# Linear attention of the third layer: a tile's head products moved into the next tile's two passes

## What is computed

```python
def gla_scan(q, k, v, loga, s0):
    ...
        b = jnp.cumsum(ac, axis=2)
        diff = b[:, :, :, None, :] - b[:, :, None, :, :]
        decay = jnp.exp(jnp.where(mask, diff, -jnp.inf))
        attn = jnp.einsum('bhid,bhjd,bhijd->bhij', qc, kc, decay)
        o = attn @ vc + jnp.einsum('bhid,bhde->bhie', qc * jnp.exp(b), S)
    ...
    o = o_f + flip(o_b)
    o = o * lax.rsqrt(jnp.mean(o * o, axis=-1, keepdims=True) + EPS)
    o = o.transpose(0, 2, 1, 3).reshape(B_, L, GLA_VAL_WIDTH) * g_gla.astype(jnp.float32)
    o = (o * jax.nn.silu(r.astype(jnp.float32))).astype(h.dtype)
```

## Time and profile before

| | us |
|---|---|
| median of 3 runs (4013.52 to 4015.33) | 4013.7 |
| the profiled execution | 4014.44 |
| its span | 4012.6 |
| PE busy in it | 3857.4 |
| DVE busy in it | 2246.1 |
| ACT busy in it | 828.2 |
| POOL busy in it | 602.2 |

### The profile page before, as it was taken

How to read it: one execution, slowest core, us unless ns; L and a number is a source line. 1 busy time by engine, 2 the same in 40 slices (tenths; PEclk the granted TensorE clock), 3 DMA queues, 4 the chain that set the end, 5 groups by cost and what they waited for, 6 DMA issues and landing times.

```text
span 4012.6 us, 45750 instructions
## 1 busy us (share of the span) xinstructions
PE 3857.4 (96%) x17426; PEld 2301.8 (57%) x17426; DVE 2246.1 (56%) x3730; ACT 828.2 (21%) x1615; POOL 602.2 (15%) x944
## 2 busy tenths in 40 slices
PE   8999999999999999999999998899999999999998
PEld 5676455544455555458744645645555444758863
DVE  0375533466566655544556016737687765438876
ACT  1265211100122222112101014521100012531000
POOL 1000000133231441400132002200000430000023
PEclk9999999999999999999999998999999999999999
DMA  5354121354412222312344112411112552002234
GB/s 190 114 203 168 32 63 53 127 178 168 141 64 74 95 69 68 126 54 94 126 168 152 58 42 93 167 38 53 63 53 75 177 179 70 9 23 84 95 126 162
DMA packets 209782, 410.57 MB, mean 102 GB/s; under 512 B 5938, under 2 KB 92296, under 8 KB 209440
## 3 DMA queue, kind: packets, MB, share of 16 engines
q1 hardware_dynamic: 203712, 386.94, 28.1%
q0 software_dynamic: 5856, 20.73, 1.7%
HBM read 405.49 MB, written 2.16 MB: 102 GB/s over the span
## 4 chain that ended last, share of the span: by engine, by line
PE 88%; DVE 6%; ACT 3%; DMA 1%; issue 1%; POOL 0%; DVEq 0%; ACTq 0%; SPq 0%; POOLq 0%
PE PS L1206 28%; PE PS L1301 19%; PE PS L1166 5%; PE PS L1139 3%; PE PS L1768 3%; PE PS L1117 3%; PE PS L1782 3%; PE PS L909 2%; PE PS L1769 1%; PE PS L1929 1%; PE PS L1939 1%; PE PS L1407 1%; PE PS L1119 1%; PE PS L1616 1%; PE PS L1418 1%
## 5 line engine op out<-in xcount | busy, mean ns | idle before, releaser
L1206 PE MATMUL PS<-UT,RING 128*128 128x384 f32 (+1 forms) x2432 | 693.8, 433 | 10.7 <-ACT BIG L2998 9.6
L1206 PEld LDWEIGHTS PS<-UT,RING 128*128 128x128 f32 x2432 | 460.9, 190 | 205.5 <-issue 15.5
L1206 PE MATMUL PS<-BIG,RING 128*128 128x384 f32 (+1 forms) x1824 | 528.5, 433 | 0.8 <-DVE BIG L2833 0.5
L1206 PEld LDWEIGHTS PS<-BIG,RING 128*128 128x128 f32 x1824 | 346.0, 190 | 147.2 <-DVEq L2004 1.1
L1301 PE MATMUL PS<-RING,BIG 128*128 128x512 f32 x810 | 377.3, 593 | 3.8 <-POOL RES_TMP L3598 1.4
L3593 POOL TENSOR_TENSOR RES_TMP<-BIG 128x128 f32<-128x128 f32 x68 | 35.7, 525 | 1668.5 <-DVE BIG L2839 581.3
L2682 DVE TENSOR_TENSOR RING<-RING 128x512 f32<-128x512 f32 x135 | 104.7, 776 | 276.5 <-DMA RING<-ff_w_dram 173.3
L1301 PEld LDWEIGHTS PS<-RING,BIG 128*128 128x128 f32 x810 | 151.2, 190 | 184.3 <-issue 177.1
L1301 PE MATMUL PS<-RING,GATE 128*128 128x512 f32 x536 | 243.9, 596 | 5.9 <-DVE RING L2685 5.9
L1301 PE MATMUL PS<-RING,RES_TMP 128*128 128x512 f32 x544 | 245.3, 593 | 1.4 <-DVE UT L2714 0.8
L1301 PEld LDWEIGHTS PS<-RING,GATE 128*128 128x128 f32 x536 | 102.0, 191 | 136.5 <-issue 125.4
(11 more groups left out here) (466 smaller groups left out, 5837.7 us busy)
## 6 DMA issues: line engine op xcount, KB each, us to landing
RING<-ff_w_dram SPq DMA_DIRECT2D x112, 1024.0 KB, 4.9
RING<-w_mod_dram SPq DMA_DIRECT2D x48, 2048.0 KB, 8.1
RING<-w_ffn_down_dram SPq DMA_DIRECT2D x55, 1024.0 KB, 5.0
RING<-w_ffn_up_dram SPq DMA_DIRECT2D x44, 1024.0 KB, 5.1
RING<-ssm_w_in_dram SPq DMA_DIRECT2D x8, 2048.0 KB, 7.8
RING<-ssm_w_out_dram SPq DMA_DIRECT2D x4, 2048.0 KB, 7.7
RING<-w_even_in_dram SPq DMA_DIRECT2D x4, 2048.0 KB, 8.6
GATE<-gates_dram POOLq DMA_DIRECT2D x12, 512.0 KB, 9.6
```

The costliest lines, as they stand in the source:

```text
L1206: m = mm(bank(bank_, n), a[:, k, :], b[:, k, :], start=k == 0, stop=k == 3)
```

## The change

`C_AT` becomes two buffers, used by even and odd tiles in turn: the old one, and `GATE[:, 1, 0, :]`. The heads of tile t are no longer one block after its second pass. They are four calls `head(t, h)` in the passes of tile t+1: after v2 and v4 of the first pass, and after v7 and v0 of the second; for tile 4 all four in the first pass of tile 5 (after v2, v3, v4, v5); for tile 5 they stay at the end. What depends on them moves later: `heads_scaled` and `heads_gated` of tile t-2 into the first pass of tile t, after v7 and v0, and `turn(t-2)` after v5 there. On DVE, P moves from a pass's end behind the copy of v7 of the next pass, and the five D of the second pass's end move between the copies, so that every pass has the same D. `mod_columns` moves from v1 to v3. ACT's steps are put in another order, with `mod_rows` ahead of part 0 of the decays for two passes later. The feed-forward gates are loaded later, after the mixer's first residual, since their place is in use; the first reader of them waits for them. DVE clears the new buffer once, in pass 0.

```diff
-        C_AT = GB[:, 1, :].rearrange("p (d h i) -> p d h i", d=2, h=4)
+        C_AT = tuple(x.rearrange("p (d h i) -> p d h i", d=2, h=4) for x in (GB[:, 1, :], GATE[:, 1, 0, :]))
...
+        def head_slots(t):
+
+            return [(0, 3), (0, 5), (1, 0), (1, 1)] if t < NT - 2 else [(0, 3), (0, 4), (0, 5), (0, 6)]
...
+                def head(t, h):
+                    if h == 0:
+                        if t == 0:
+                            pe.wait_ge(S("L2_states_ready"), 1)
+                        pe.wait_ge(S("L2_attention_ready"), 2 * t + 2)
+                        go_bank[t] = 4 + place(go)
+                    b = go_bank[t]
+                    rows, a = slice((h % 2) * 64, (h % 2) * 64 + 64), h // 2
+                    ops = [(C_AT[t % 2][:, dr, h % 2 * 2 + a, :], C_V[:, t, h * 128:(h + 1) * 128]) for dr in range(2)]
+                    ops += [(C_QB[rows, 2 * dr + a, t * 128:(t + 1) * 128], C_S[rows, dr * 6 + t, a * 128:(a + 1) * 128])
+                            for dr in range(2) if t != first[dr]]
+                    for j, (x, y) in enumerate(ops):
+                        m = mm(bank(b + h % 2, 128, a * 128), x, y, start=j == 0, stop=j == len(ops) - 1)
+                    if h == GLA_H - 1:
+                        m.then_inc(go.full, 1)
...
-                            if v_ == 1 and 2 in next_of and t + dr:
+                            if v_ == 3 and 2 in next_of and t + dr:
                                 mod_columns(3, 2 * t + dr - 1, 7, MOD_ROWS[2])
+                            if t and (dr, i) in head_slots(t - 1):
+                                head(t - 1, head_slots(t - 1).index((dr, i)))
+                            if i == 6 and dr == 0 and t >= 2:
+                                turn(t - 2)
...
-                    if t:
-                        dve.wait_ge(go.full, t)
+                    if t >= 2:
+                        dve.wait_ge(go.full, t - 1)
...
-                        if dr == 1 and v_ in (7, 0, 1) and n + 1 < 2 * NT:
+                        if n and v_ == 7:
+                            products(n, 1)
+                        if n and v_ in (7, 0, 1) and n + 1 < 2 * NT:
                             differences(n + 1, [4 + (v_ + 1) % 8])
...
-                        if dr == 0 and v_ in (4, 5) and n + 2 < 2 * NT:
+                        if v_ in (4, 5) and n + 2 < 2 * NT:
                             differences(n + 2, [v_ - 2])
-                        if dr == 1 and v_ == 4 and t:
-                            heads_scaled(t - 1)
-                        if dr == 1 and v_ == 5 and t:
-                            heads_gated(t - 1)
+                        if n == 0 and v_ == 4:
+                            step(V.memset(GATE[:, 1, 0, :], 0.0))
+                        if dr == 0 and v_ == 7 and t >= 2:
+                            heads_scaled(t - 2)
+                        if dr == 0 and v_ == 0 and t >= 2:
+                            heads_gated(t - 2)
...
                     post("L2_attention_ready")
-                    if n + 1 < 2 * NT:
-                        products(n + 1, 1)
-                    if dr == 1 and n + 2 < 2 * NT:
-                        differences(n + 2, range(2, 7))
...
+                    if n and n + 1 < 2 * NT:
+                        level_decays(n + 1, 1)
                     if n and 2 in next_of:
                         mod_columns(3, n - 1, 7)
-                    if dr == 1 and n + 1 < 2 * NT:
-                        level_decays(n + 1, 1)
-                    if dr == 0 and n + 2 < 2 * NT:
-                        level_decays(n + 2, 0)
+                    if t and (dr == 1 or t == NT - 1) and n < 2 * NT - 1:
+                        head_roots(t - 1)
+                    if dr == 0 and t >= 2:
+                        turned(t - 2)
                     if 2 in next_of:
                         mod_rows(3, n, 7, MOD_ROWS[2])
-                    if dr == 1 and n + 2 < 2 * NT:
+                    if n + 2 < 2 * NT:
                         level_decays(n + 2, 0)
...
-                    spread_gates(L)
+                    spread_gates(L, (0,))
...
+                    if L == 2:
+                        spread_gates(L, (1,))
```

More of the change, by code:

```diff
@@ L1551, in turn @@
                     m.then_inc(gt.full, 1)
+                first = [o[0] for o in gla_orders()]
+                go_bank = {}
+                def head(t, h):
[13 more added lines that the diff above has]
+                        m.then_inc(go.full, 1)
                 for t in range(NT):
                     for dr in range(2):
-                        for v_ in LEVEL_ORDER:
+                        for i, v_ in enumerate(LEVEL_ORDER):
                             if v_ in (0, 4):
@@ L1566, in mixer2 @@
                             m.then_inc(lv.full, 1)
-                            if v_ == 1 and 2 in next_of and t + dr:
+                            if v_ == 3 and 2 in next_of and t + dr:
                                 mod_columns(3, 2 * t + dr - 1, 7, MOD_ROWS[2])
+                            if t and (dr, i) in head_slots(t - 1):
+                                head(t - 1, head_slots(t - 1).index((dr, i)))
+                            if i == 6 and dr == 0 and t >= 2:
+                                turn(t - 2)
                         if 2 in next_of:
                             mod_rows(3, 2 * t + dr, 7)
-                    if t:
-                        turn(t - 1)
-                    if t == 0:
-                        pe.wait_ge(S("L2_states_ready"), 1)
-                    pe.wait_ge(S("L2_attention_ready"), 2 * t + 2)
-                    b = 4 + place(go)
-                    first = [o[0] for o in gla_orders()]
-                    for h in range(GLA_H):
-                        rows, a = slice((h % 2) * 64, (h % 2) * 64 + 64), h // 2
-                        ops = [(C_AT[:, dr, h % 2 * 2 + a, :], C_V[:, t, h * 128:(h + 1) * 128]) for dr in range(2)]
-                        ops += [(C_QB[rows, 2 * dr + a, t * 128:(t + 1) * 128], C_S[rows, dr * 6 + t, a * 128:(a + 1) * 128])
-                                for dr in range(2) if t != first[dr]]
-                        for j, (x, y) in enumerate(ops):
-                            m = mm(bank(b + h % 2, 128, a * 128), x, y, start=j == 0, stop=j == len(ops) - 1)
-                    m.then_inc(go.full, 1)
+                turn(NT - 2)
+                for h in range(GLA_H):
+                    head(NT - 1, h)
                 if 2 in next_of:
@@ L2721, in added @@
                 def added(q, tile, h):
-                    if (L, q, tile, h) == (0, 0, 0, 0):
-                        dve.wait_ge(S("gates_in"), gates_so_far(0))
+                    if L in (0, 2) and (q, tile, h) == (0, 0, 0):
+                        dve.wait_ge(S("gates_in"), gates_so_far(L))
                     t, hs = 2 * q + tile, slice(h * 512, (h + 1) * 512)
@@ L2864, in _ @@
                 (mixer0, mixer1, mixer2, mixer3)[L]()
[L2865 removed]
+                dve.wait_ge(S("gates_in"), gates_so_far(L) - (32 if L in (0, 2) else 0))
                 n = 2 if L == 1 else 1
@@ L3274, in turned, with head_roots @@
                     give(gt, A(C_MIX[:, 4:8, t * 128:(t + 1) * 128], bank(6).rearrange("p (a b) -> p a b", a=4), ACT.Copy))
+                def head_roots(t):
+                    act.wait_ge(go.full, t + 1)
+                    for h in range(GLA_H):
+                        step(A(C_JUNK, bank(4 + h % 2, 128, h // 2 * 128), ACT.Square, accum_out=ST2[:, 32 + h:33 + h]))
+                    step(A(ST2[:, 36:40], ST2[:, 32:36], ACT.Sqrt, scale=1.0 / GLA_DV, bias=EPSC))
+                    post("head_rms_ready")
                 for n in range(2):
@@ L3280, in mixer2 @@
                     t, dr = n // 2, n % 2
+                    if n and n + 1 < 2 * NT:
+                        level_decays(n + 1, 1)
                     if n and 2 in next_of:
                         mod_columns(3, n - 1, 7)
[L3283 to L3286 removed]
+                    if t and (dr == 1 or t == NT - 1) and n < 2 * NT - 1:
+                        head_roots(t - 1)
+                    if dr == 0 and t >= 2:
+                        turned(t - 2)
                     if 2 in next_of:
                         mod_rows(3, n, 7, MOD_ROWS[2])
[L3289 removed]
+                    if n + 2 < 2 * NT:
                         level_decays(n + 2, 0)
[L3291 to L3300 removed]
+                turned(NT - 2)
+                head_roots(NT - 1)
                 if 2 in next_of:
```

18 lines of the change are left out of this document (5 added, 13 removed).

## The result

The changed kernel takes 4023.66 us (median of 17 runs; 16 of them lie between 4009.66 and 4032.39) against 4014.68 for the kernel before on the same chip (17 runs, 4011.02 to 4017.94): 1.002 times as long, 95% interval 1.0013 to 1.0026. It is slower, by 9 us, where 5 us less was forecast, and it lies outside the range. It is also less steady: its 16 runs are spread over 23 us, those of before over 7. One execution took 5964.3 us at a granted clock of 0.633; it fell in a slower state of the chip and counts neither in the spread nor in the ratio, and without it the median is 4023.49.

The account below looks back on a forecast made before the run. PE and DVE handing work to and fro bound the levels: 149.35 us becomes 141.1, 8.2 less; two clock falls take back 3.2, leaving 5.0: 4013.7 - 5.0 = 4008.7 us, own range 4004.5 to 4013, eight-in-ten range 4002.5 to 4016.0.

Parts of the forecast that it names:

- The bound and the terms: Stretch of the levels: PE and DVE hand work to and fro; pass lengths sum to 141.1 us against 149.35.
- rival 1: Levels: nearly all the gain holds, or more; without falls 8.2 us less, time 4005.5; chance 0.22.
- the signs named: Levels: v7 copies 10.6 to 14.2 us apart, no L922 wait for ACT, DVE waiting 0.8 to 1.5 at pass ends.
- rival 2: Start of each pass: PE waits at v0 because ACT's decays come late, most of the gain gone, 4012.7; chance 0.06.
- rival 3: Between DVE's copies: D, P and POOL's copies block each other, each D 0.28 us longer, time 4015.7; chance 0.03.
- What takes part of it back: the clock: Passes 4, 6, 8, 10: PE's quiet stretch lets its clock fall to half, taking back 3.2 of 8.2 us.
- The count: Passes 4, 6, 8, 10: two clock falls assumed, as in the kernel before.
- My upper bound of four: Clock falls in all of passes 4, 6, 8 and 10, costing 4 x 2.6 = 10.4 us.
- The price: Chain at a pass's end: a fall costs 1.6 us for `mod_rows`, about 1 more for a head; rows alone taken.
- Rival 5: Clock falls in all four of passes 4, 6, 8 and 10, 2.2 us slower, time 4015.9; chance 0.05.
- Rival 4: Clock stays at half through the middle of passes 2 to 11, stretch 166 us, time 4030; chance 0.04.
- the 0.71 of the earlier trace: Kernel before, 2546 to 2548: PE busy 0.71 of 2 us, some microseconds before its clock was halved.

Follow-up runs that it names:

- filler behind v1: Changed kernel plus eight products that nothing reads (the filler) on PE behind v1 of every even pass from tile 1 on: 4006.74 us.
- filler behind v5: Changed kernel plus the same eight unread products, but behind v5 of the even passes, where PE is busy anyway: 4028.66 us.
- the second profile: Profile of the changed kernel measured again without an edit, on another batch's chip: median 4022.79 us; also called changed again.
- 15.9 with filler: Kernel before plus four unread products each behind v0 and v1 of the odd passes: 4012.47 us.
- four heads in one pass: Changed kernel with all four heads of every tile in the first pass of the next tile, instead of two and two: 4023.14 us.
- P back: Changed kernel with P put back behind the last copy of the pass before, ahead of the next v7 copy: 4007.58 us.
- four idle products a pass: Changed kernel with P back, plus four unread products behind v1 of the even passes: 4001.55 us.
- rows moved: Changed kernel with `mod_rows` of each odd pass but the last, and ACT's copy of it, moved behind v1 of the next pass: 4006.61 us.
- two edits: Changed kernel with rows moved and P back together: 4013.59 us, against 4013.78 for the kernel before on the same chip.

## Why the prediction was wrong

**The bound and the terms: right.** With the costly falls taken away by filler, the twelve passes measured 140.7, forecast 141.1; the largest error in one pass is 0.27 (pass 0). In part errors cancel: pass 2, forecast 11.3, took 10.9 in the profile in which it had neither filler nor fall, and 11.5 with filler, which doesn't fit whole into its wait of 1.33. "At no fall 8.2, time 4005.5" was rival 1; the kernel that realises it came out at 4006.74, 7.9 less than before on its chip. (Rival 1 compares an order without falls with one that has them: 3.0 of its 8.2 are the old order's own, as above.) Of the signs named, the odd passes are 10.8 (10.9 forecast; over 11.5 would have meant a missing term), L922 waits nowhere for ACT's copy of the rows, and DVE waits for PE at a pass's end: 0.8 and 1.4 with filler behind v1, as forecast, and up to 2.4 in the changed kernel (first row of DVE above), since the chain ahead was at half clock.

**No wait for ACT (rival 2), no blocking of D and POOL (rival 3): right.** Either would lengthen the passes of the kernel with filler too, and they are as forecast. The reading that D isn't slower beside POOL's copies was too good, though: it takes 0.42 or 0.43 where POOL is idle, and beside POOL's copies mostly 0.54 in the new order and 0.43 to 0.55 in the old. That is 0.1 more, and not the 0.28 of rival 3.

**"What takes part of it back: the clock" is the step that failed.** It had the mechanism and the place (PE nearly idle from 0.4 to 3.9 in passes 4, 6, 8 and 10), and was mis-sized twice.
- The count. I took two falls, as before. There were six that cost time, in passes 2, 3, 4, 6, 8 and 10 (lengths beside those with filler: +4.0, +1.6, +1.4, +6.0, +1.3, +1.4), and one in pass 1 that cost none. My upper bound of four left out passes 2 and 3. Pass 3 has no wait of 2 us; its fall came behind levels that keep PE busy for half to three quarters of each microsecond, which in passes 5, 7 and 9 went by without a fall.
- The price. I priced a fall at 1.6, `mod_rows` alone, bound 2.6. Before, that was the price: passes 7 and 9 lost 1.4 and 1.7, and their `mod_rows` 1.3 and 1.6, since the levels behind the gap ran slow under DVE's cover. In the new even passes PE's whole chain, two heads, four levels, `turn` and `mod_rows`, stands behind the gap; pass 6 lost 6.0, and in the kernel with filler behind v5 4.5 were lost although `mod_rows` ran at full speed.

Together 15.7 us in the profile and 17 between the medians, in place of 3.2. The forecast's 8.2, with the 0.4 by which the structure came out better, less 15.7 is -7.1, the loss of the stretch (the same numbers in another order, so no proof of their own).

Rival 5 had the mechanism, with four falls of 2.6 each (4015.9); the average of the six was 2.6 as well. Rival 4, half clock through the middle of the passes (4030), is what pass 6 shows, and passes 4, 6, 8 and 10 in the second profile; the median of 4023.66 lies between the two. They had 0.05 and 0.04. The chance of rival 5 leaned on "the slow `mod_rows` before were in two of the five second passes that had such a stretch". But the slow rows undercount the falls: before, the clock fell in pass 3 as well, at no cost (16.0 us, 15.9 with filler), so in three of the five. And those gaps had a level in their middle. Before, in tile 3, on both sides of the 0.71 of the earlier trace rows, and the uncounted fall in tile 1:

```profile
2498.00:2500.00 2.00, 2.00 (x22) 1.88 (x18) 1.53 (x3) 1.69 (x2) 0.00 (x0) 0.51 1.05 407
...
2544.00:2546.00 2.00, 1.03 (x16) 0.84 (x16) 1.65 (x2) 1.98 (x6) 0.79 (x4) 1.00 0.38 65
...
2548.00:2550.00 2.00, 1.86 (x19) 1.48 (x21) 0.98 (x3) 1.30 (x4) 0.00 (x0) 0.81 1.05 410
```

The new ones are a wait of 2.25 us in one piece. It shows as two thin windows in a row (pass 6, above) or as one with nothing in it (pass 4, while DVE does P, D and the scaling), by where the edges of the windows fall; the wait is the same:

```profile
2508.00:2510.00 2.00, 0.00 (x0) 0.00 (x0) 1.79 (x5) 1.97 (x3) 1.67 (x6) 1.00 1.02 369
...
2512.00:2514.00 2.00, 2.00 (x15) 1.55 (x16) 1.79 (x4) 1.54 (x2) 0.00 (x0) 0.52 0.53 195
```

```profile
2510.22 0.72 PE L1588 MATMUL PS<-UT 64*128 64x128 f32 x8 [2.25 <-DVE GB L2401]
```

The rule of the Trainium skill that the prediction weighed ("TensorE: Matmul & The Clock Gate", section "A second HAM failure mode: psum-queue depth-cycling") says that short, frequent idling between groups of products makes the clock fall and rise again. The trace agrees in the main: the clock fell behind the gap in all five even passes from pass 2 on, where the forecast set this aside as a rival. It isn't bound to, though: behind the same gap it held in one, three and four of the five in three other profiles (changed again, filler behind v5, four heads in one pass).

## What to carry to other kernels

When work moves out of a block into the cover of another engine, look at what is left for PE in the place that it comes to wait in, not only at who waits for whom: a new gap of 2 us, free by itself, cost nothing where the clock held and 1.3 to 6.0 us where it fell. As an upper bound, price a fall by all of PE's chain up to where it next has cover, not by one instruction. Count the falls by the granted clock, not by one slow instruction, which shows neither a fall under cover nor one that ends before it. Where the gap can't be closed by needed work, products that nobody reads close it: one edit (P back) and four idle products a pass are worth 21 us here against the changed kernel, and 13.6 against the one before. Not all of it is the clock: the profiled stretch is 137.5 there and 140.7 with filler alone, so that some 3 come from the place of P.

## What the runs showed of the hardware

- Behind the same wait of 2.25 us, with the same levels around it, PE ran at 1.2 GHz for some 13 us without a gap of its own (pass 6) or for about 3 (pass 4), and in other profiles it kept its 2.4 GHz. What decides between a short and a long fall, and whether one comes at all (pass 2: 15.5 in one profile, 10.9 in the other), is open.
- The same 16 passes over the array cost nothing when they stood in PE's gap of 2.25 us (pass 10 takes 14.1 with them and, at full clock in the kernel with four heads in one pass, without) and 1.8 us a pass on its chain.
- The changed kernel's spread of 18 to 23 us goes with its clock (0.991 in the shortest of the first 16 runs, 0.983 in the longest); the kernels with few costly falls in their profile (filler behind v1, P back with and without filler, rows moved) lie within 4 to 9 us. A narrow spread is no proof of the contrary: the five runs with filler behind v5, with two falls of 4.5, lie within 2 us.
- Removing one gap can uncover the next: two edits that each won 7 to 8 us won 0.2 together.
